# Feed-forward entry of a two-layer decoder: token halves as even and odd tiles, first products in two parts, second weight tile's work reordered

## The chip, the cores and the metric

The kernel runs on one core of a Trainium2 chip. The metric is the device time of one execution in microseconds; the median of the runs is compared, and lower is better. All 1024 tokens and all weights are float32; the products are made from rounded parts (a high part and the remainder) of each operand.

## The reference

Two layers over 1024 tokens of width 1024. The first mixes tokens by pooling, the second by sliding-window attention; what the change touches is the entry of each layer's feed-forward part.

```python
def swiglu(x, w_gate, w_up, w_down):
    return (jax.nn.silu(x @ w_gate) * (x @ w_up)) @ w_down

    for i in range(DEPTH):
        hn = rms_norm(h, mix_pre_g[i])
        ...
        h = h + rms_norm(m, mix_post_g[i])
        f = swiglu(rms_norm(h, ffn_pre_g[i]), w_ff_gate[i], w_ff_up[i], w_ff_down[i])
        h = h + rms_norm(f, ffn_post_g[i])
        gate = jax.nn.sigmoid(rms_norm(h, ple_norm_g[i]) @ w_ple_gate[i])
        h = h + (p[i] @ w_ple_proj[i]) * gate
```

## The kernel before

The token axis has eight tiles of 128 (numbered 0 to 7, in pairs `i` with `p` = 0, 1). All of them stay on chip in `H`. Of the feed-forward part, gate and up projections together are computed by a seven-product scheme of the Strassen kind: the token axis, the contraction axis and gate/up are each cut into halves, and seven products replace eight. Each product (`ffn_product`) takes one form of the weights (A11, A12, A22, S1 to S4; A21 is only a summand) and one form of the activations: b11, b21, b22 are parts of the turned, normed tiles, t1 to t4 are differences of them. A form of the activations has four pieces of 128 tokens, so a product is 4 x 3 matmuls of 512 columns (high x high, high x remainder, remainder x high). A11 and A12 need b11 and b21, that is one token half only; every other form but b22 needs both halves.

The hidden axis of 2816 is walked in 11 groups `g` of two weight tiles `t` (0 and 1). For each group the loop makes seven products per weight tile and then two sets of 14 products of the down projection (`ffn_pe_down`), beside the next group's work. Group 0 has no down projection beside it. The first weight tile (0, 0) is written out by itself (`ffn_pe_first`, `ffn_act_first`, `ffn_dve_first`, `ffn_pool_first`), since its products lie between the last tiles of the stage before.

In that stage (pooling in layer 0, the output projection in layer 1) each tile passes: product on TensorE; squares of the output on ScalarE (`output_squares`, L595); the root on GpSimd; scaling and residual add on VectorE (`add_post`, L473, L476); squares of the residual (`fn_squares`, L493); root on GpSimd (`fn_rms`); norm into `tmp` (`fn_normed`, L507); a turn on TensorE into banks 6 and 7 (`fn_turn`, L518); copies (`fn_raw`), rounding (`fn_hi`) and remainders (`fn_lo`). In the kernel before, tiles 0 to 3 are the first token half and need only copy, rounding and two remainders; tiles 4 to 7 are the second, and each makes on VectorE two differences (L568, L569), a third (L575), b22's remainder (L579) and a fourth difference (L585). So A11 and A12 of the first weight tile can run before tiles 6 and 7 are turned, and all other products wait for tile 7.

The order of work on each engine is the order in the code; engines wait for each other by counted semaphores. TensorE's order at the entry (`ffn_pe_first`): A11, turn of tile 6, A12, turn of tile 7, twelve filler matmuls (`keep_busy`, L841), S3, S2, S1, A22, S4; before it, a priming matmul (L835) in bank 1, 2 and 5 opens each bank that several products add to. `copy_first` copies A11's bank on ScalarE so that A12 and the others may be added to either copy; `copy_m7` copies the bank of S3, `copy_u` that of S2. Then `ffn_pe_tile` does the second weight tile in the order A11, S3, S2, A12, S1, A22, S4.

A weight form is loaded raw by SP (L789), summed where it is a sum (`form_sum`, L1111, VectorE or GpSimd), rounded by ScalarE (`form_hi`, L978), and its remainder taken by VectorE or GpSimd (`form_lo`, L1162), which writes over the raw form. The down weights get four sums (`wd_sums`, L1140 to L1146), rounding (`wd_his`, L990) and remainders (`wd_los`, L1155) on the same engines; the activations that come out of the products get their own forms (`d_sums`, L1206 to L1214; `d_his`; `d_los`, from L1223). The down projection's first product of group 0 (L924) needs all of these. Forms of t are rounded by `t_hi` (L1035) and their remainders made by `t_lo` (L1261).

## Time and profile before

| | us |
|---|---|
| median of 3 runs | 1965.93 |
| lowest, highest | 1965.68, 1967.02 |
| the profiled execution | 1965.92 |
| its span in the profile | 1964.1 |

| engine | busy us | share |
|---|---|---|
| TensorE, matmul | 1917.4 | 98% |
| TensorE, weight load | 1573.6 | 80% |
| VectorE | 1402.6 | 71% |
| ScalarE | 905.4 | 46% |
| GpSimd | 457.5 | 23% |

In rows of a timeline the first number is the start from the beginning of the span, the second the time from the first start to the last end of what the row merges, and in brackets stands how long the engine was idle before it and what released it. Instructions overlap at their ends, so the cost of one in a stream is read from start to start. PE is TensorE, DVE VectorE, ACT ScalarE, POOL GpSimd.

### The profile page before, as it was taken

The page shows a single profiled execution, that of the slowest core. Times are in us where ns is not written, and L with a number is a line of the kernel's source. Part 1 is how long each engine was busy: PE and PEld are TensorE (multiplying, and loading weights), DVE is VectorE, ACT ScalarE, POOL GpSimd, SP SyncE. Part 2 cuts the span into 40 slices and gives each one's busy share as a digit, 9 for nine tenths or more (in the row PEclk, how much of TensorE's full clock was granted, in tenths as well). Part 3 has the DMA queues.
Part 4 walks back from the last instruction along what each step waited for, and adds up shares of the span by engine and source line. Part 5 has one row for each costly group of instructions (what it writes and reads, how often), then busy time and mean ns, then how long its engine had stood idle before and what let it go on. Part 6 is the DMA issues. An engine that isn't in the chain of part 4 may idle for free.

```text
span 1964.1 us, 28703 instructions
## 1 busy us (share of the span) xinstructions
PE 1917.4 (98%) x9198; PEld 1573.6 (80%) x9198; DVE 1402.6 (71%) x2382; ACT 905.4 (46%) x1734; POOL 457.5 (23%) x448
## 2 busy tenths in 40 slices
PE   7899999999999999999999999999999999999998
PEld 7778888888888878888866787788888888888787
DVE  5987777777777786565389658777777777777863
ACT  6744444444444453341178545444444444444531
POOL 2312222222222221010046211212122221222310
PEclk9999999999999999999999999999999999999999
DMA  5333332233333350254200213233333223335201
GB/s 201 108 97 104 91 91 87 76 102 91 107 91 91 92 200 22 78 219 172 86 12 2 66 42 123 71 107 92 98 94 91 86 75 106 91 106 176 99 30 67
DMA packets 222055, 188.50 MB, mean 96 GB/s; under 512 B 12192, under 2 KB 199968, under 8 KB 221984
## 3 DMA queue, kind: packets, MB, share of 16 engines
q1 hardware_dynamic: 217712, 183.38, 29.2%
q10 hardware_dynamic: 4272, 4.21, 0.7%
q8 instruction: 40, 0.66, 0.1%
q14 instruction: 31, 0.25, 0.0%
HBM read 166.58 MB, written 20.97 MB: 95 GB/s over the span
## 4 chain that ended last, share of the span: by engine, by line
PE 89%; DVE 6%; issue 2%; ACT 1%; DMA 1%; POOL 1%; SPq 0%; DVEq 0%; ACTq 0%; POOLq 0%
PE ps L827 14%; PE ps L829 14%; PE ps L828 14%; PE ps L315 7%; PE ps L317 7%; PE ps L316 7%; PE ps L925 7%; PE ps L926 7%; PE ps L924 7%; PE ps L1635 2%; PE ps L1716 1%; PE ps L1689 1%; PE ps L389 1%; PE ps L632 1%; DVE t_lo L1261 1%
## 5 line engine op out<-in xcount | busy, mean ns | idle before, releaser
L1249 DVE TENSOR_TENSOR H<-H,ps 128x512 f32<-128x512 f32 x496 | 328.0, 686 | 112.5 <-PE ps L926 111.7
L1111 POOL TENSOR_TENSOR s_raw<-s_raw,a_raw 128x512 f32<-128x512 f32 x66 | 87.5, 1327 | 766.4 <-DVE s_lo L1162 651.0
L827 PE MATMUL ps<-t_hi,s_hi 128*128 128x512 f32 x528 | 206.4, 391 | 8.1 <-DVE t_lo L1261 5.1
L828 PE MATMUL ps<-t_lo,s_hi 128*128 128x512 f32 x528 | 205.5, 389 | 0.0
L829 PE MATMUL ps<-t_hi,s_lo 128*128 128x512 f32 x528 | 205.5, 389 | 0.0
L1000 ACT ACTIVATE m<-ps 128x512 f32<-128x512 f32 x44 | 26.4, 600 | 265.7 <-PE ps L829 263.3
L827 PE MATMUL ps<-b_hi,a_hi 128*128 128x512 f32 x352 | 137.4, 390 | 0.0
L828 PE MATMUL ps<-b_lo,a_hi 128*128 128x512 f32 x352 | 137.3, 390 | 0.0
L829 PE MATMUL ps<-b_hi,a_lo 128*128 128x512 f32 x352 | 137.2, 390 | 0.0
L924 PE MATMUL ps<-wd_hi,d_ab_hi 128*128 128x512 f32 x336 | 130.7, 389 | 0.0
L925 PE MATMUL ps<-wd_lo,d_ab_hi 128*128 128x512 f32 x336 | 130.7, 389 | 0.0
L926 PE MATMUL ps<-wd_hi,d_ab_lo 128*128 128x512 f32 x336 | 130.7, 389 | 0.0
L827 PEld LDWEIGHTS ps<-t_hi,s_hi 128*128 128x128 f32 x528 | 99.1, 188 | 31.4 <-DVE t_lo L1261 6.8
L829 PEld LDWEIGHTS ps<-t_hi,s_lo 128*128 128x128 f32 x528 | 99.1, 188 | 20.8
L828 PEld LDWEIGHTS ps<-t_lo,s_hi 128*128 128x128 f32 x528 | 99.1, 188 | 20.4
L978 ACT ACTIVATE s_hi<-s_raw 128x512 fp32r<-128x512 f32 x132 | 82.8, 627 | 53.9 <-DVE s_raw L1111 53.9
L1162 POOL TENSOR_TENSOR a_lo<-a_raw,a_hi 128x512 fp32r<-128x512 f32 x60 | 80.8, 1347 | 114.2 <-ACT a_hi L978 114.2
L315 PE MATMUL ps<-w_ple_gate_hi,xt_hi 128*128 128x512 f32 x256 | 101.5, 397 | 1.8 <-DVE w_ple_gate_lo L291 0.8
L317 PE MATMUL ps<-w_ple_gate_hi,xt_lo 128*128 128x512 f32 x256 | 99.9, 390 | 0.0
L316 PE MATMUL ps<-w_ple_gate_lo,xt_hi 128*128 128x512 f32 x256 | 99.7, 389 | 0.0
L941 ACT ACTIVATE ps<-ps 128x512 f32<-128x512 f32 x88 | 51.2, 582 | 97.6 <-PE ps L926 90.8
L1681 POOL TENSOR_TENSOR probs<-probs,recip 128x1024 f32<-128x1024 f32 x32 | 60.6, 1893 | 147.8 <-DVE recip L1673 147.8
(293 smaller groups left out, 5022.8 us busy)
## 6 DMA issues: line engine op xcount, KB each, us to landing
a_raw<-in_w_ff_gate SPq DMA_DIRECT2D x88, 256.0 KB, 2.9
a_raw<-in_w_ff_up SPq DMA_DIRECT2D x88, 256.0 KB, 3.0
s_raw<-in_w_ff_up SPq DMA_DIRECT2D x88, 256.0 KB, 2.9
s_raw<-in_w_ff_gate SPq DMA_DIRECT2D x88, 256.0 KB, 3.1
wd_raw<-in_w_ff_down SPq DMA_DIRECT2D x44, 512.0 KB, 4.3
residual_spill<-H SPq DMA_DIRECT2D x16, 512.0 KB, 2.6
raw<-in_w_ple_gate SPq DMA_DIRECT2D x16, 512.0 KB, 6.0
back<-residual_spill SPq DMA_DIRECT2D x16, 512.0 KB, 5.8
```

The costliest lines, as they stand in the source:

```text
L315: pe.matmul(out_, lhs[0], rhs[0], start=first, stop=False)
L316: pe.matmul(out_, lhs[0], rhs[1], start=False, stop=False)
L317: return pe.matmul(out_, lhs[1], rhs[0], start=False, stop=last)
L827: pe.matmul(ps[:, bank, :], w[0], x[0], start=fresh and k == 0, stop=False, skip_group_check=not fresh)
L828: pe.matmul(ps[:, bank, :], w[0], x[1], start=False, stop=False, skip_group_check=not fresh)
L829: last = pe.matmul(ps[:, bank, :], w[1], x[0], start=False, stop=k == 3, skip_group_check=not fresh)
L924: pe.matmul(ps[:, bank, :], a[0], wd_hi[:, b, :], start=fresh, stop=False, skip_group_check=not fresh)
L925: pe.matmul(ps[:, bank, :], a[0], wd_lo[:, b, :], start=False, stop=False, skip_group_check=not fresh)
L926: pe.matmul(ps[:, bank, :], a[1], wd_hi[:, b, :], start=False, stop=True, skip_group_check=not fresh).then_inc(F["down"], 1)
L978: act.activation(W[name][0][:, :, :], form_raw(name), ACT.Copy).then_inc(F["form_hi"], 1)
L1111: eng.tensor_tensor(form_raw(name), W_RAW[name][:, :, :], form_raw(other) if other != "A21" else W_RAW["A21"][:, :, :], op).then_inc(summe ...
L1249: dve.tensor_tensor(dst, dst, src, ALU.add).then_inc(F["summed"], 1)
```

## The change

The token halves become the even tiles (b11, b21) and the odd tiles (b22 and the differences), so a pair 2i, 2i + 1 completes piece i of each form. For group 0 the orders of products, roundings and remainders are written out for both weight tiles together (`ENTRY`, `ENTRY_HI`, `ENTRY_LO`, from which the semaphore counts follow). A11 and A12 of weight tile (0, 0) and A11 of (0, 1) are done in two parts, three pieces (384 columns) before tile 6 is ready and one piece (128 columns) after it; A12 of (0, 1) follows whole, all before S3. The filler matmuls of this place are gone. The second weight tile uses its own banks (`bank_for`) and, for A11, A12 and the raw S1, its own places (`ahead_hi`, `ahead_lo`, `ahead_raw`), loaded by SP when tile 7's product of the stage before is done. Its remaining products are S2, S3, S1, A22, S4 (`ffn_pe_second`), and on ScalarE and VectorE its own copies, roundings and sums stand ahead of the down weights' (`ffn_act_second`, `ffn_dve_second`). t2 is rounded in one pass instead of two. In layer 0 the squares of tile 7 stand ahead of tile 6's copy, in layer 1 behind it. The additions to `H`, the spills' return, the per-layer-embedding stage and the output follow the new tile order through `rows_of`. The number of products is the same. The diff, cut to its core (lines of white space are left out):

```diff
 ORDER = ("A11", "S3", "S2", "A12", "S1", "A22", "S4")
-ORDER_FIRST = ("A11", "A12", "S3", "S2", "S1", "A22", "S4")
+ENTRY = (("A11 begun", 0), ("A11", 0), ("A12", 0), ("A11", 1), ("A12", 1), ("S3", 0), ("S2", 0), ("S1", 0), ("A22", 0), ("S4", 0),
+         ("S2", 1), ("S3", 1), ("S1", 1), ("A22", 1), ("S4", 1))
...
             pe.wait_ge(FN["xn"], done(n))
-            if 1 <= 2 * i + p <= 4:
-                pe.wait_ge(FN["raw"], 1 + 4 * L + 2 * i + p)
+            if p == 1:
+                pe.wait_ge(FN["raw"], 1 + 4 * L + i + 1)
             else:
                 pe.wait_ge(FN["lo"], free(n))
             for k in range(KD):
...
+            if p == 0:
+                act.activation(piece(t_raw[1], i), ps[:, 6, :], ACT.Copy)
+                act.activation(piece(t_raw[4], i), ps[:, 7, :], ACT.Copy).then_inc(FN["raw"], 1)
             else:
-                act.activation(piece(t_raw[3], n - 4), ps[:, 6, :], ACT.Copy)
-                act.activation(piece(xb["b22"][0], n - 4), ps[:, 7, :], ACT.Copy).then_inc(FN["hi"], 1)
+                act.activation(piece(t_raw[3], i), ps[:, 6, :], ACT.Copy)
+                act.activation(piece(xb["b22"][0], i), ps[:, 7, :], ACT.Copy).then_inc(FN["hi"], 1)
         def fn_hi(act, L, i, p):
-            n = 2 * i + p
-            if n < 4:
-                act.wait_ge(FN["raw"], 1 + 4 * L + n + 1)
-                act.activation(piece(xb["b11"][0], n), piece(t_raw[1], n), ACT.Copy)
-                act.activation(piece(xb["b21"][0], n), piece(t_raw[4], n), ACT.Copy).then_inc(FN["hi"], 1)
+            if p == 0:
+                act.wait_ge(FN["raw"], 1 + 4 * L + i + 1)
+                act.activation(piece(xb["b11"][0], i), piece(t_raw[1], i), ACT.Copy)
+                act.activation(piece(xb["b21"][0], i), piece(t_raw[4], i), ACT.Copy).then_inc(FN["hi"], 1)
         def fn_lo(dve, L, i, p):
             n = 2 * i + p
             dve.wait_ge(FN["hi"], done(TILES * L + n))
-            if n < 4:
+            if p == 0:
                 for form, held in (("b11", 1), ("b21", 4)):
-                    hi, lo = [piece(x, n) for x in xb[form]]
-                    last = dve.tensor_tensor(lo, piece(t_raw[held], n), hi.bitcast(F32), ALU.subtract)
+                    hi, lo = [piece(x, i) for x in xb[form]]
+                    last = dve.tensor_tensor(lo, piece(t_raw[held], i), hi.bitcast(F32), ALU.subtract)
                 last.then_inc(FN["lo"], 1)
             else:
                 fn_two_forms(dve, L, n)
...
+        def as_form(x):
+            return x.rearrange("p a c -> p (a c)").rearrange("p (k c) -> p k c", k=4)
+        ahead_hi = {"A11": as_form(Z["d_ac_hi"][:, :, :]), "A12": as_form(Z["d_ab_lo"][:, 0:2, :])}
+        ahead_lo = {"A11": as_form(Z["d_ac_lo"][:, :, :]), "A12": as_form(Z["d_ab_lo"][:, 2:4, :])}
+        ahead_raw = {"A11": as_form(Z["d_ac_raw"][:, :, :]), "A12": as_form(Z["d_ab_raw"][:, 2:4, :]),
+                     "S1": as_form(Z["s1_ahead"][:, 0:2, :])}
...
+        def bank_for(b, g, t):
+            if is_first(g, t):
+                return 4 if b == 3 else b
+            if is_second(g, t):
+                return 3 if b == 0 else b + 4
+            return b
         m7, up0_last, act_late = Z["m7"], Z["up0_last"], ACT_LATE
...
-                pe.matmul(ps[:, bank, :], w[0], x[1], start=False, stop=False, skip_group_check=not fresh)
-                last = pe.matmul(ps[:, bank, :], w[1], x[0], start=False, stop=k == 3, skip_group_check=not fresh)
-            last.then_inc(F["product"], 1)
-        def ffn_pe_prime(pe, form, *primed):
+                w, x = [y[:, k, :] for y in forms_], [y[:, pieces, k, :] for y in X[name]]
+                pe.matmul(o, w[0], x[0], start=fresh and k == 0, stop=False, skip_group_check=not fresh)
+                pe.matmul(o, w[0], x[1], start=False, stop=False, skip_group_check=not fresh)
+                last = pe.matmul(o, w[1], x[0], start=False, stop=k == 3, skip_group_check=not fresh)
+            if pieces.stop == 4 or (name == "A11" and is_first(g, t)):
+                last.then_inc(F["product"], 1)
+        def ffn_pe_prime(pe, form, pieces, *primed):
             for bank in primed:
-                pe.matmul(ps[:, bank, :], W[form][0][:, 0, :], X[form][0][:, :, 0, :], start=True, stop=True)
+                pe.matmul(ps[:, bank, pieces.start * P:pieces.stop * P], W[form][0][:, 0, :], X[form][0][:, pieces, 0, :],
+                          start=pieces.start == 0, stop=True, skip_group_check=pieces.start > 0)
         def keep_busy(pe, count, bank):
@@ -843,18 +888,34 @@
         def ffn_pe_first(pe, L):
             g, t, s = 0, 0, S[("pool", "o")[L]]
+            early, late = slice(0, 3), slice(3, 4)
             pe.wait_ge(*ready("A11", L, g, t))
+            pe.wait_ge(FN["lo"], done(TILES * L + 4))
             if L == 1:
                 pe.wait_ge(FN["ssum"], done(TILES * L + TILES - 2))
-            ffn_pe_prime(pe, "A11", 1)
-            ffn_product(pe, "A11", L, g, t)
-            fn_turn(pe, L, PAIRS - 1, 0)
+            if L == 1:
+                fn_turn(pe, L, PAIRS - 1, 0)
+            ffn_pe_prime(pe, "A11", early, 1)
+            ffn_product(pe, "A11", L, g, t, early)
             pe.wait_ge(s["added"][0], s.done("added", PAIRS - 1))
-            ffn_pe_prime(pe, "A12", 2)
+            pe.wait_ge(*ready("A12", L, g, t))
+            ffn_pe_prime(pe, "A12", early, 2)
+            pe.wait_ge(F["copied"], copied_early(L))
+            ffn_product(pe, "A12", L, g, t, early)
+            if L == 0:
+                fn_turn(pe, L, PAIRS - 1, 0)
+            ffn_product(pe, "A11", L, 0, 1, early)
+            pe.wait_ge(FN["lo"], done(TILES * L + TILES - 2))
+            ffn_pe_prime(pe, "A12", late, 1, 2)
+            ffn_product(pe, "A11", L, g, t, late)
+            pe.wait_ge(s["added"][1], s.done("added", PAIRS - 1))
+            ffn_pe_prime(pe, "A12", slice(0, 4), 5)
+            fn_turn(pe, L, PAIRS - 1, 1)
             pe.wait_ge(F["copied"], nth_copy(0, L, g, t))
-            ffn_product(pe, "A12", L, g, t)
-            fn_turn(pe, L, PAIRS - 1, 1)
-            keep_busy(pe, 12, 3)
+            ffn_product(pe, "A12", L, g, t, late)
+            ffn_product(pe, "A11", L, 0, 1, late)
+            pe.wait_ge(F["copied"], nth_copy(0, L, 0, 1))
+            ffn_product(pe, "A12", L, 0, 1)
             pe.wait_ge(F["t"], 4 * L + 1)
             ffn_product(pe, "S3", L, g, t)
             pe.wait_ge(F["t"], 4 * L + 2)
@@ -866,8 +927,19 @@
             ffn_product(pe, "A22", L, g, t)
             pe.wait_ge(FN["lo"], done(TILES * L + TILES - 1))
             pe.wait_ge(F["up1"], 1 + tau(L, g, t) + 1)
-            pe.wait_ge(*ready("S4", L, g, t))
-            ffn_pe_prime(pe, "S4", 5)
+            ffn_product(pe, "S4", L, g, t)
+        def ffn_pe_second(pe, L):
+            g, t = 0, 1
+            pe.wait_ge(*ready("S2", L, g, t))
+            ffn_pe_prime(pe, "S2", slice(0, 4), 6)
+            for name in ("S2", "S3"):
+                ffn_product(pe, name, L, g, t)
+            pe.wait_ge(F["copied"], nth_copy(2, L, g, t))
+            for name in ("S1", "A22"):
+                ffn_product(pe, name, L, g, t)
+            pe.wait_ge(F["up1"], 1 + tau(L, g, t) + 1)
             ffn_product(pe, "S4", L, g, t)
...
@@ -1022,24 +1108,35 @@
         def ffn_act_first(act, L):
             g, t = 0, 0
-            copy_first(act, L, g, t)
+            if L == 1:
+                fn_raw(act, L, PAIRS - 1, 0)
+            copy_first(act, L, g, t, "A11 begun")
             if L == 0:
                 first_hi(act, L)
-            fn_raw(act, L, PAIRS - 1, 0)
+                form_hi(act, "A11", L, 0, 1)
+            else:
+                fn_hi(act, L, PAIRS - 1, 0)
             fn_squares(act, L, PAIRS - 1, 1)
+            if L == 0:
+                fn_raw(act, L, PAIRS - 1, 0)
+                fn_hi(act, L, PAIRS - 1, 0)
+            else:
+                form_hi(act, "A11", L, 0, 1)
+            form_hi(act, "A12", L, 0, 1)
+            copy_first(act, L, g, t)
             def t_hi(m, pieces):
-                n = pieces.stop + 3
+                n = 2 * pieces.stop - 1
                 act.wait_ge(t_step, steps_of(L, n) + {3: 1, 1: 2, 2: 3, 4: 4}[m])
                 act.activation(xb[f"t{m}"][0][:, pieces, :, :], t_raw[m][:, pieces, :, :], ACT.Copy
                                ).then_inc(F["t_hi"], 1)
-            for m in (3, 2):
-                t_hi(m, slice(0, 3))
+            t_hi(3, slice(0, 3))
             fn_raw(act, L, PAIRS - 1, 1)
-            for m in (3, 2):
-                t_hi(m, slice(3, 4))
+            copy_first(act, L, 0, 1)
+            t_hi(3, slice(3, 4))
+            t_hi(2, slice(0, 4))
             t_hi(1, slice(0, 4))
             form_hi(act, "A22", L, g, t)
             copy_m7(act, L, g, t)
@@ -1048,13 +1145,12 @@
             form_hi(act, "S4", L, g, t)
             gate_silu(act, L, g, t, 0)
             n = following(g, t)
-            for name in ("A11", "S3", "S2", "A12", "S1"):
+            for name in ("S3", "S2", "S1"):
                 form_hi(act, name, L, *n)
         def ffn_act_tile(act, L, g):
-            t, p, n, down = 0, preceding(g, 0), following(g, 0), g - 1
-            gate_silu(act, L, *p, 1)
+            t, n, down = 0, following(g, 0), g - 1
             form_hi(act, "S2", L, g, t)
             d_his(act, L, down, 0)
...
+            if is_second(g, t):
+                copy_u(act, L, g, t)
+                copy_m7(act, L, g, t)
+                form_hi(act, "A22", L, g, t)
+                form_hi(act, "S4", L, g, t)
+                wd_his(act, L, g, range(4))
+            else:
+                wd_his(act, L, g, (0, 1))
+                copy_first(act, L, g, t)
+                form_hi(act, "A22", L, g, t)
+                wd_his(act, L, g, (2, 3))
+                copy_m7(act, L, g, t)
+                form_hi(act, "S4", L, g, t)
+                copy_u(act, L, g, t)
             if not is_last(g, t):
                 form_hi(act, "A11", L, *n)
             gate_silu(act, L, g, t, 0)
             if not is_last(g, t):
                 form_hi(act, "S3", L, *n)
+                gate_silu(act, L, g, t, 1)
...
                                          ALU.subtract)
             last = steps_of(L, TILES - 1)
+            if L == 0:
+                form_lo(dve, "A11", L, 0, 1)
             fn_lo(dve, L, PAIRS - 1, 0)
+            if L == 1:
+                form_lo(dve, "A11", L, 0, 1)
             fn_normed(dve, L, PAIRS - 1, 1)
+            form_lo(dve, "A12", L, 0, 1)
             if L == 0:
                 form_lo(dve, "S3", L, g, t)
-            fn_fourth_form(dve, L, TILES - 2)
             t_lo(3, slice(0, 3), 1, last)
             dve.wait_ge(FN["hi"], done(TILES * L + TILES - 1))
             fn_two_forms(dve, L, TILES - 1)
-            t_lo(3, slice(3, 4), 3, last + 1).then_inc(F["t"], 1)
+            t_lo(3, slice(3, 4), 2, last + 1).then_inc(F["t"], 1)
             fn_second_form(dve, L, TILES - 1)
             fn_fourth_form(dve, L, TILES - 1)
             if L == 0:
                 form_lo(dve, "S2", L, g, t)
-            t_lo(2, slice(0, 4), 4, last + 4).then_inc(F["t"], 1)
+            t_lo(2, slice(0, 4), 3, last + 4).then_inc(F["t"], 1)
             if L == 0:
                 form_lo(dve, "S1", L, g, t)
-            t_lo(1, slice(0, 4), 5, last + 4).then_inc(F["t"], 1)
...
+            if is_second(g, t):
+                times_up(dve, L, *p, 1)
+                form_sum(dve, "S4", L, g, t)
+                form_lo(dve, "A22", L, g, t)
+                wd_sums(dve, L, g)
+                form_lo(dve, "S4", L, g, t)
+                up_second_half(dve, L, g, t)
+                wd_los(dve, L, g, (0, 1))
+                up_first_half(dve, L, g, t)
+                times_up(dve, L, g, t, 0)
+                form_lo(dve, "A11", L, *n)
+                form_sum(dve, "S3", L, *n)
+                wd_los(dve, L, g, (2, 3))
+                form_sum(dve, "S1", L, *n)
+                form_sum(dve, "S2", L, *n)
+                form_lo(dve, "S3", L, *n)
+                d_sums(dve, L, g, 0)
+                return
             wd_sums(dve, L, g)
             times_up(dve, L, *p, 1)
...
+            return 2 * (slot % 4) + slot // 4
+        def slot_rows(i, p):
+            return bass.ds(rows_of(2 * i + p) * D, D)
         def of_tile(work, L):
...
+                sp.wait_ge(s["used"][1], s.done("used", PAIRS - 1))
+                ffn_load(sp, "A11", "a11", L, 0, 1)
+                ffn_load(sp, "A12", "a12", L, 0, 1)
                 spill_tile(5)
                 spill_tile(6)
+                sp.wait_ge(s["added"][1], s.done("added", PAIRS - 1))
+                ffn_load(sp, "S4", "a12", L, *first)
                 sp.wait_ge(FN["ssum"], done(TILES * L + TILES - 1))
                 ffn_load(sp, "A22", "a22", L, *first)
+                sp.wait_ge(F["form_loaded"]["S1"], 16 * (tau(L, 0, 0) + 1))
+                ffn_load(sp, "S1", "a22", L, 0, 1)
                 spill_tile(TILES - 1)
-                ffn_load(sp, "S4", "a12", L, *first)
                 ffn_load_down(sp, L, 0)
                 for t in range(2):
                     ffn_load_tile(sp, L, 0, t)
```

## Rows read from the trace of the kernel before

**Rows 1.** The page's head and its part on busy time.

```profile
span 1964.1 us, 28703 instructions
...
PE 1917.4 (98%) x9198; PEld 1573.6 (80%) x9198; DVE 1402.6 (71%) x2382; ACT 905.4 (46%) x1734; POOL 457.5 (23%) x448
```

**Rows 2.** TensorE's waits over the span: releaser, total us, times, longest.

```profile
engine line waited for: us in total, times, longest us
...
PE ps L518 <- DVE tmp L507: 6.5, 4, 2.7
...
PE ps L827 <- DVE t_lo L1261: 5.1, 5, 1.3
```

**Rows 3.** Timeline, TensorE, layer 0's entry: start us, us, instruction, idle before.

```profile
80.14 1.67 PE L518 MATMUL ps<-ident,tmp 128*128 128x128 f32 x8 [2.68 <-DVE tmp L507]
...
86.91 1.10 PE L518 MATMUL ps<-ident,tmp 128*128 128x128 f32 x8 [1.09 <-DVE tmp L507]
...
87.85 2.84 PE L841 MATMUL ps<-ident 128*128 128x128 f32 x24
...
91.97 0.50 PE L827 MATMUL ps<-t_hi,s_hi 128*128 128x512 f32 x1 [1.28 <-DVE t_lo L1261]
...
115.45 0.50 PE L827 MATMUL ps<-t_hi,s_hi 128*128 128x512 f32 x1 [0.94 <-ACT ps L1005]
...
126.48 0.39 PE L827 MATMUL ps<-b_hi,s_hi 128*128 128x512 f32 x1
...
134.64 0.39 PE L924 MATMUL ps<-wd_hi,d_ac_hi 128*128 128x512 f32 x1
```

**Rows 4.** Timeline, TensorE, layer 1's entry.

```profile
1201.55 1.09 PE L518 MATMUL ps<-ident,tmp 128*128 128x128 f32 x8 [2.17 <-DVE tmp L507]
...
1210.31 0.50 PE L827 MATMUL ps<-t_hi,s_hi 128*128 128x512 f32 x1 [0.67 <-DVE t_lo L1261]
...
1214.04 0.47 PE L827 MATMUL ps<-t_hi,s_hi 128*128 128x512 f32 x1 [0.72 <-issue]
...
1248.64 0.39 PE L924 MATMUL ps<-wd_hi,d_ac_hi 128*128 128x512 f32 x1
```

**Rows 5.** A stretch of TensorE, layer 0: length, PE busy, granted clock, DMA.

```profile
80.00:83.70 3.70, 3.56 (x13) 0.57 0.00 0
```

**Rows 6.** Timelines, VectorE and ScalarE, layer 1's entry.

```profile
1196.56 1.22 DVE L476 TENSOR_TENSOR H<-H,ps 128x1024 f32<-128x1024 f32 x1
...
1197.88 1.07 ACT L493 ACTIVATE o_junk<-H 128x1024 f32<-128x1024 f32 x1 [0.33 <-DVE H L476]
...
1198.93 2.84 ACT L1035 ACTIVATE t_hi<-t_raw 128x1536 fp32r<-128x1536 f32 x2
...
1207.97 4.49 DVE L1261 TENSOR_TENSOR t_lo<-t_raw,t_hi 128x2048 fp32r<-128x2048 f32 x2
```

**Rows 7.** Timeline, VectorE, layer 1, second weight tile.

```profile
1225.38 0.69 DVE L1140 TENSOR_TENSOR wd_raw<-wd_raw 128x512 f32<-128x512 f32 x1
...
1228.11 0.69 DVE L1189 TENSOR_TENSOR act_late<-m,act_late 128x512 f32<-128x512 f32 x1
...
1230.58 2.35 DVE L1155 TENSOR_TENSOR wd_lo<-wd_raw,wd_hi 128x1024 fp32r<-128x1024 f32 x2
...
1232.85 0.68 DVE L1111 TENSOR_TENSOR s_raw<-s_raw,a_raw 128x512 f32<-128x512 f32 x1
...
1233.45 1.82 DVE L1155 TENSOR_TENSOR wd_lo<-wd_raw,wd_hi 128x1024 fp32r<-128x1024 f32 x2
...
1242.08 0.69 DVE L1111 TENSOR_TENSOR s_raw<-s_raw,a_raw 128x512 f32<-128x512 f32 x1
...
1244.28 0.42 DVE L1206 TENSOR_TENSOR d_ac_raw<-d_ab_raw 128x256 f32<-128x256 f32 x1
...
1246.47 0.69 DVE L1223 TENSOR_TENSOR d_ac_lo<-d_ac_raw,d_ac_hi 128x512 fp32r<-128x512 f32 x1
```

**Rows 8.** Timelines, VectorE and GpSimd, layer 0.

```profile
62.03 1.29 DVE L507 SCALAR_TENSOR_TENSOR tmp<-H,small,gain 128x1024 f32<-128x1024 f32 x1 [1.08 <-POOL small L501]
...
93.98 3.22 POOL L1111 TENSOR_TENSOR s_raw<-s_raw,a_raw 128x512 f32<-128x512 f32 x1 [8.69 <-issue]
```

166 lines of the change are left out of this document (94 added, 72 removed), and 3 rows, old and new, of the table ENTRY_LO.

## The prediction

> **What bounds the kernel now.** I read the busy times first, then TensorE's waits, then the timeline around both entries of the feed-forward part, then the two engines that feed it. TensorE has work for 1917.4 of 1964.1 us [rows 1], so about 47 us of idle time is all that a reordering can win; a change here must be judged by TensorE's start times. The waits put two of the larger sums at the entry: the turns of the normed tiles (6.5 us in four waits) and the products on the combined forms (5.1 us) [rows 2]. The timeline shows the same picture in both layers. In layer 0 the turn of tile 6 waits 2.68 us and that of tile 7 1.09, twelve filler matmuls (24 instructions) run for 2.84, S3 waits another 1.28, and the second weight tile stalls 0.94 on a copy [rows 3]. In layer 1 tile 7's turn waits 2.17 [rows 4]. From 126.48 to 134.64 TensorE does three products without a gap [rows 3]: 2.72 us per product of twelve 512-column matmuls, 0.227 each. That stretch ends in the first product of the down projection, and so I take its start (134.64 and 1248.64) as the finish line: behind it the loop is untouched.
>
> **The change: what leaves TensorE's path.** Pairing even with odd tiles makes the combined forms late by one quarter only, and A11 and A12 can start on three quarters. The filler is gone, A11 and A12 of the second weight tile (5.44 us) move up in front of S3, and the second tile's stall goes, since S2 now opens it and S3 covers the copy. If these were all, layer 1 would win some 6 us. Each step must be followed to what is late next, because the added work is itself waiting for something.
>
> **The entry in layer 1.** Up to the residual add of tile 7 nothing on the path moves; that add starts at 1196.56 and is 1.22 long, so it ends at 1197.78 [rows 6].
> 1. Squares of tile 7: 0.10 later, 1.15 with the accumulator read, to 1199.03 (before: 1197.88 to 1198.93) [rows 6]. Only then does ScalarE round A11 of tile two, 0.6, and VectorE takes the remainder, 0.7 with the hand-over: ready at 1200.35.
> 2. TensorE has by then done turn 6, A11 and A12 on three quarters, and stands from about 1198.4: a wait of 2 us that replaces the 2.17 in front of the turn.
> 3. A11 of tile two on 384 columns: 12 x 0.17 (three quarters of 0.227) = 2.04. Then 14 matmuls of 128 columns. No row has this form; the nearest is the filler, also 128 wide and with its own weight loads, 24 in 2.84 = 0.118 [rows 3], against a floor of a quarter of 0.227 and a ceiling of the whole. I take 0.12, since the filler's weight loads are of the same size: 1.7. A priming matmul 0.23. The turn of tile 7 starts at 1204.3, where it was 1201.55 [rows 4]: 2.75 later.
> 4. ScalarE copies the last quarter of A11 and rounds three quarters of t3 (half of 2.84 [rows 6]) before it reads the turn: its copy ends at 1207.0. VectorE: the rest of t3's remainder, two differences 1.2, then t3's last quarter 0.7 behind a rounding of 0.6, the third difference at 1210.6.
> 5. t2 was rounded in two parts, so that only a quarter (0.5) stood on the path; now all four quarters are one pass behind the last tile, 1.85, and its remainder 2.25 (two of that size took 4.49 [rows 6]). S2 can start at 1214.95, where it was 1210.31 [rows 4]: 4.64 later. TensorE's own order (12 + 12 narrow, A12 of tile two, S3) ends at 1214.3, so the two chains are nearly equal and one replaces the other.
> The price of moving the loads: A11 and A12 of tile two are issued when tile 7's product has read its operands, 3 us or more before they are rounded, so no one waits for them; the two spills that SP now issues behind them are needed only at the first down additions. The sum for S4 on GpSimd waits for S2's remainder; the loads of A21 and S3 are queued behind it on SP, and are wanted 10 us later.
>
> **The second weight tile.** From S2: to S1 3.73 as before (1210.31 to 1214.04 [rows 4]), then S1, A22, S4 8.2, restart and priming 0.3, S2 and S3 of tile two 5.45, drain 0.15: S3 ends 17.85 after S2's start, at 1232.8. By TensorE alone S1, A22, S4 and the next group's A11 and S3 follow, 13.6, and the down product would start at 1246.4, 2.2 earlier than before.
> But the vector side no longer keeps up. ScalarE copies S3's bank before it rounds A22, so VectorE's remainder of A22 waits for the end of S3 plus 1.18; and everything of the down weights is queued behind that remainder on VectorE, where before the four sums of wd began at 1225.38, ahead of it [rows 7]. From there: remainder of A22, of S4, up's second half, the next A11 and the sum S3, five passes of 0.60; up's first half and its product 1.4; the sums of wd 2.73 (1225.38 to 1228.11); remainders of wd 2.27 for four slots (1230.58 to 1232.85) and 1.7 for three; sums S1, S2 and remainder of S3 2.2 (1242.08 to 1244.28) [rows 7]. That is 13.3. The forms of the activations and the first remainder add 2.9 (1244.28 to 1246.47, plus 0.69) [rows 7]. So the down product starts 1.18 + 13.3 + 2.9 = 17.4 behind S3's end, not 13.6: at 1250.2, against 1248.64. On the way the next A11 waits about 2 us and the next S3 about 1.7. Layer 1: +1.6.
>
> **The entry in layer 0.** The odd tiles' four passes now fall on tiles 1 and 3. Tile 1's go into waits; tile 3's 2.5 us meet a wait of 1.08 [rows 8], so the last pool product starts 0.5 later, and tile 7's residual add, with the reordered tail, ends at 83.9 in place of 83.1. Then the order differs: squares to 85.2, and only behind them the copy and rounding of tile 6 (1.0 + 1.1) to 87.3, its remainders 1.2 to 88.6, A11's last quarter to 90.35, turn 7 at 90.6 (it was 86.91 [rows 3]); then the same chain as above, to a remainder of t2 that starts at 98.8. GpSimd's sum for S4 now comes in front of that one; in the profile it shared the ports for 3.22 us [rows 8], undisturbed sums take 1.3, and I charge 0.6 (bounds 0 and 1.9). S2 at 101.75, the down product 35.4 later (17.85 + 17.4, and 0.15 because this layer's S1 restarts slower): 137.2, against 134.64 [rows 3]. Layer 0: +2.6. TensorE's clock fell to 0.57 of full speed, near the lower of its two levels (1.2 GHz), after the wait of 2.68 [rows 5]; there are again waits of 2 to 2.7 us, but the slowed matmuls would lie ahead of another wait (for tile 6's remainders), so I charge nothing; uncovered it costs up to 1.8.
>
> **Sum.** The profiled execution took 1965.92 us, equal to the median of 1965.93, with 1.8 of it outside the span. 1965.9 + 1.6 + 2.6 = 1970.1. All else (the PLE part and the output in another tile order, the loads back, the key and value stage, whose tile k needs a slot no later than k + 3) is the same number of instructions with slack, and I cost it at nothing.
>
> The Trainium skill ("TensorE: Matmul & The Clock Gate", Back-to-back issue gap) gives about 81 ns for a 128-column matmul in a stream of weight load and matmul. No row here has such a matmul of this data type. By that figure turn 7 comes 0.55 earlier in each layer, and the sum would be 1969.0.
>
> **Rivals.**
> A, the forecast: VectorE bounds the second tile, 1970.1; its own range is 1967 to 1972. For it: the program order of the two queues leaves no choice. Chance 0.47.
> B, narrow matmuls cost as much as wide ones: 0.227 at 128 columns. Turn 7 then comes 1.5 later, and the 24 behind it take 2.6 more, so that TensorE's own order gets ahead of t2; S2 is 3.4 later in each layer: 1970.1 + 6.8 = 1976.9. Against it: the filler's 0.118. Chance 0.18.
> C, the faster side: VectorE keeps up in the second tile. It decides whether A22's rounding really waits for S3's end; if A22's remainder comes 3.9 us sooner, TensorE's 13.6 counts. Then layer 1 ends 2.2 earlier than before and layer 0 1.4 earlier: 1965.9 - 3.6 = 1962.3. For it: VectorE has over 2 us of waiting in that stretch. Against it: both queues are strict in order. Chance 0.17.
> D, the entry is shorter than I sum, by 2 us a layer, while the second tile stays bound: 1966. For it: my chain has some twenty hand-overs. Chance 0.18.
>
> **How the numbers follow.** The predicted time is A's, 1970.1. The range 1962.3 to 1977 takes in C's and B's times and leaves their outer halves out, about 2 in 10. A measurement of this kernel tells 0.2% (3.9 us) from no change. Slower by more than that (over 1969.9): 0.28 of A and all of B but a little, 0.46. Faster (under 1962.0): half of C and a little of D, 0.12. Within: the rest, 0.42.
>
> **What the new profile would show.** Right: the first down product near 137 and 1250; idle time of 1.5 to 2 us in front of the next group's A11 and again S3, released by VectorE; in front of A11 of tile two a wait of 2 to 3 us; the turns of tile 7 near 90.6 and 1204.3. The price of 128 columns can be read from start to start. Wrong would be: a second tile without waits (C), or the last quarter of A11 taking 2.7 us (B).

## Result and the profile after

The changed kernel takes 1972.62 us, the median of six executions (1970.18 to 1975.68); the kernel before took 1966.26 beside it (1965.68 to 1967.02). The ratio is 1.0032, with a 95% interval of 1.0022 to 1.0043: 6.4 us slower. The forecast was 1970.1. The profiled execution is the fastest of the six, 1970.18, with a span of 1968.3 against 1964.1 [rows 1]. So the result has two parts that must be read apart: 4.2 us that the profile holds, and a spread upwards that it does not. Five more executions of the same kernel took 1972.67 to 1975.56.

The page of the changed kernel, busy times, and TensorE's waits (releaser, total us, times, longest); they answer to [rows 1] and [rows 2]:

```profile
PE 1919.2 (98%) x9228; PEld 1576.6 (80%) x9228; DVE 1404.5 (71%) x2382; ACT 905.0 (46%) x1734; POOL 453.6 (23%) x448
...
PE ps L870 <- DVE d_ac_lo L1268: 4.1, 2, 2.5
PE ps L870 <- DVE s_lo L1268: 3.0, 2, 1.5
...
PE ps L870 <- DVE a_lo L1268: 2.5, 2, 1.3
...
PE ps L870 <- DVE t_lo L1367: 1.4, 2, 1.0
...
PE ps L528 <- DVE tmp L517: 0.5, 2, 0.3
```

The 6.5 us in front of the turns are down to 0.5, and the 5.1 in front of the combined forms to 1.4. In their place stand 4.1 us in front of A11 of tile two (`d_ac_lo` holds its lower half; I call a form's rounded part its upper half and the remainder its lower half), and 3.0 and 2.5 us in front of the next group's S3 and A11.

TensorE's timeline, changed kernel, layer 0 and then layer 1 (start us, us, instruction, idle before and its releaser), beside [rows 3] and [rows 4]:

```profile
80.98 1.04 PE L528 MATMUL ps<-ident,tmp 128*128 128x128 f32 x8
84.54 0.45 PE L870 MATMUL ps<-b_hi,d_ac_hi 128*128 128x384 f32 x1 [2.52 <-DVE d_ac_lo L1268]
84.83 0.34 PE L871 MATMUL ps<-b_lo,d_ac_hi 128*128 128x384 f32 x1
85.00 0.35 PE L872 MATMUL ps<-b_hi,d_ac_lo 128*128 128x384 f32 x1
...
85.75 0.52 PE L872 MATMUL ps<-b_hi,d_ac_lo 128*128 128x384 f32 x1
86.07 0.52 PE L870 MATMUL ps<-b_hi,d_ac_hi 128*128 128x384 f32 x1
...
88.66 0.44 PE L879 MATMUL ps<-b_hi,a_hi 128*128 128x128 f32 x2 [0.47 <-DVE b_lo L562]
88.94 0.27 PE L870 MATMUL ps<-b_hi,a_hi 128*128 128x128 f32 x1
89.05 0.28 PE L871 MATMUL ps<-b_lo,a_hi 128*128 128x128 f32 x1
...
90.56 1.04 PE L528 MATMUL ps<-ident,tmp 128*128 128x128 f32 x8
...
101.67 0.50 PE L870 MATMUL ps<-t_hi,s_hi 128*128 128x512 f32 x1 [1.04 <-DVE t_lo L1367]
...
129.68 0.50 PE L870 MATMUL ps<-b_hi,a_hi 128*128 128x512 f32 x1 [1.23 <-DVE a_lo L1268]
134.21 0.50 PE L870 MATMUL ps<-t_hi,s_hi 128*128 128x512 f32 x1 [1.48 <-DVE s_lo L1268]
137.11 0.39 PE L996 MATMUL ps<-wd_hi,d_ac_hi 128*128 128x512 f32 x1
```

```profile
1194.99 1.04 PE L528 MATMUL ps<-ident,tmp 128*128 128x128 f32 x8
...
1202.87 0.45 PE L870 MATMUL ps<-b_hi,d_ac_hi 128*128 128x384 f32 x1 [1.63 <-DVE d_ac_lo L1268]
1206.88 1.03 PE L528 MATMUL ps<-ident,tmp 128*128 128x128 f32 x8
1217.36 0.50 PE L870 MATMUL ps<-t_hi,s_hi 128*128 128x512 f32 x1 [0.39 <-DVE t_lo L1367]
1252.81 0.39 PE L996 MATMUL ps<-wd_hi,d_ac_hi 128*128 128x512 f32 x1
```

The finish lines move from 134.64 [rows 3] to 137.11, +2.47, and from 1248.64 [rows 4] to 1252.81, +4.17, of which 1.70 arise in layer 1. That is the whole difference of the spans.

Between executions, layer 0 starts some tenths earlier or later. So below I count from the turn of tile 6 to the first down product of the same layer: 56.13 us in layer 0 (80.98 to 137.11) and 57.82 in layer 1 (1194.99 to 1252.81) in the changed kernel. I call them the stretches.

VectorE's timeline, changed kernel, layer 0, second weight tile:

```profile
116.91 0.69 DVE L1216 TENSOR_TENSOR s_raw<-s_raw,a_raw 128x512 f32<-128x512 f32 x1 [1.67 <-DMA s_raw<-in_w_ff_gate]
120.73 0.69 DVE L1268 TENSOR_TENSOR a_lo<-a_raw,a_hi 128x512 fp32r<-128x512 f32 x1 [3.13 <-ACT a_hi L1050]
...
136.26 0.69 DVE L1329 TENSOR_TENSOR d_ac_lo<-d_ac_raw,d_ac_hi 128x512 fp32r<-128x512 f32 x1
```

VectorE stands still for 3.13 us in front of A22's lower half and then has no gap until the forms of the activations at 136.26: the down product cannot start before that.

### The profile page after: what moved, and what is told of

Same layout as the page of the kernel before. It is cut to its first block, busy times and chain, and to the rows that moved or that the text cites. A ratio compares the mean times of both kernels' runs of the same rounds, so it can differ in the third digit from the quotient of the medians.

```text
span 1968.3 us, 28728 instructions
## 1 busy us (share of the span) xinstructions
PE 1919.2 (98%) x9228; PEld 1576.6 (80%) x9228; DVE 1404.5 (71%) x2382; ACT 905.0 (46%) x1734; POOL 453.6 (23%) x448
## 4 chain that ended last, share of the span: by engine, by line
PE 89%; DVE 6%; ACT 2%; issue 2%; POOL 1%; DMA 0%; POOLq 0%; DVEq 0%; ACTq 0%
PE ps L870 14%; PE ps L872 14%; PE ps L871 14%; PE ps L325 7%; PE ps L327 7%; PE ps L326 7%; PE ps L998 7%; PE ps L997 7%; PE ps L996 7%; PE ps L1769 2%; PE ps L1850 1%; PE ps L1823 1%; PE ps L399 1%; PE ps L641 1%; DVE w_ple_gate_lo L301 1%
## 5 line engine op out<-in xcount | busy, mean ns | idle before, releaser
L870 PE MATMUL ps<-b_hi,a_hi 128*128 128x512 f32 (+2 forms) x352 | 134.8, 383 | 4.0 <-DVE a_lo L1268 2.5
L871 PE MATMUL ps<-b_lo,a_hi 128*128 128x512 f32 (+2 forms) x352 | 134.3, 382 | 0.0
L872 PE MATMUL ps<-b_hi,a_lo 128*128 128x512 f32 (+2 forms) x352 | 134.3, 382 | 0.0
```

The lines of the kernel that those rows point to most:

```text
L870: pe.matmul(o, w[0], x[0], start=fresh and k == 0, stop=False, skip_group_check=not fresh)
L871: pe.matmul(o, w[0], x[1], start=False, stop=False, skip_group_check=not fresh)
L872: last = pe.matmul(o, w[1], x[0], start=False, stop=k == 3, skip_group_check=not fresh)
```

## Experiments: VectorE's queue in the second weight tile

My theory: in the second tile, what counts is VectorE's queue, and it starts late because ScalarE copies S3's bank ahead of rounding A22. The rival was that copies and SiLU on ScalarE are the chain and VectorE only follows.

**e1.** The rounding of A22 goes ahead of both copies that wait for TensorE, that of S4 ahead of the copy of S3's bank.

```
 if is_second(g, t):
+    form_hi(act, "A22", L, g, t)
     copy_u(act, L, g, t)
-    copy_m7(act, L, g, t)
-    form_hi(act, "A22", L, g, t)
     form_hi(act, "S4", L, g, t)
+    copy_m7(act, L, g, t)
     wd_his(act, L, g, range(4))
```

> In the second tile ScalarE rounds A22 ahead of both PSUM copies, and S4 ahead of the copy from S3's bank; the order of VectorE and TensorE stays. Theory M (between S3 of tile two and the first down product VectorE's queue is the bound, and it stands still 3.1 us in each layer in front of A22's second half because ScalarE reaches A22's first half only after S3's copy): the wait of VectorE before A22's lower half goes from 3.1 to under 0.5 us, the waits before the next A11 and the next S3 (1.2 and 1.5 us) vanish, the first down products come 2.5 to 3 us earlier in each layer (at 134.1 to 134.6 in layer 0), and the time is 5 to 6 us below that of the changed kernel, at or below the kernel before. Rival C' (VectorE only waits for what is late anyway, the bound is ScalarE's own chain of copy and SiLU): the wait moves, the down products come within 0.5 us of 137.1 and 1252.8.

Measured: median 1969.32, from 1965.62 to 1971.41 over eleven executions. Its profile, VectorE in layer 0 and TensorE in layer 1:

```profile
122.08 0.69 DVE L1216 TENSOR_TENSOR s_raw<-s_raw,a_raw 128x512 f32<-128x512 f32 x1 [1.58 <-DMA s_raw<-in_w_ff_gate]
122.69 0.68 DVE L1268 TENSOR_TENSOR a_lo<-a_raw,a_hi 128x512 fp32r<-128x512 f32 x1
```

```profile
1198.14 1.04 PE L528 MATMUL ps<-ident,tmp 128*128 128x128 f32 x8
...
1250.67 0.50 PE L870 MATMUL ps<-t_hi,s_hi 128*128 128x512 f32 x1 [1.43 <-DVE s_lo L1268]
1253.52 0.44 PE L996 MATMUL ps<-wd_hi,d_ac_hi 128*128 128x512 f32 x1
```

The 3.1 us of standing still are gone, and layer 1's stretch goes from 57.82 to 55.38: 2.44 less, a little under the 2.5 to 3 expected, since VectorE now waits 0.75 us for TensorE in front of up's second half. Layer 0 of this execution ran at a low clock (below), so its stretch, 58.68, can't be compared. The fastest execution is at 1965.62, 4.6 below the changed kernel's; I had expected 5 to 6. The theory holds against its rival, with one part wrong: the wait in front of the next A11 vanished, that in front of the next S3 (1.43) stayed. The order of two queues in the second tile is thus worth more than the 4.2 us by which the change is slower.

**e5.** On top of e1, VectorE's sums of the down weights go ahead of S4's sum, where it waited 1.58 us for a load. The first rounding of them (two slots) goes on ScalarE ahead of the copy of S3's bank, and its remainder on VectorE ahead of up's second half.

```
 form_hi(act, "S4", L, g, t)
+wd_his(act, L, g, (0,))
 copy_m7(act, L, g, t)
-wd_his(act, L, g, range(4))
+wd_his(act, L, g, (1, 2, 3))
...
-form_sum(dve, "S4", L, g, t)
-form_lo(dve, "A22", L, g, t)
 wd_sums(dve, L, g)
+form_sum(dve, "S4", L, g, t)
+form_lo(dve, "A22", L, g, t)
 form_lo(dve, "S4", L, g, t)
+wd_los(dve, L, g, (0,))
 up_second_half(dve, L, g, t)
-wd_los(dve, L, g, (0, 1))
+wd_los(dve, L, g, (1,))
 up_first_half(dve, L, g, t)
```

> On top of the ScalarE order of e1, VectorE forms the sums of the down weights ahead of S4's sum of tile two, where it waited 1.6 us for a load, and ScalarE and VectorE round the first two of them ahead of S3's copy and the last sum of the tile. Theory M (in the second tile VectorE's queue is the bound to the end, and each us that it stands still ahead of it is worth a us): the wait before the next S3, 1.4 us in both layers in e1, falls under 0.4, the first down product of layer 1 comes 1.1 to 1.4 us earlier than in e1 counted from the turn of tile 6 (55.4 to about 54.1 us), and the fastest executions go from 1965.6 to about 1963. Rival (the wait before S3 is set by SiLU and the sums behind it): it stays at 1.4. The spread of 5 us from the clock stays.

Measured: median 1967.23 (1964.81 to 1970.51), stretch of layer 1 55.27, so 0.1 less and not 1.1 to 1.4; the wait before the next S3 is 1.28. (The medians of e1 and e5 differ by 2.1 us, but both kernels spread over more than 5, so I go by the stretches.) Its VectorE, layer 0:

```profile
124.12 0.69 DVE L1279 TENSOR_TENSOR act_late<-ps,m 128x512 f32<-128x512 f32 x1 [0.82 <-PE ps L872]
...
126.84 0.69 DVE L1285 TENSOR_TENSOR m<-ps,m 128x512 f32<-128x512 f32 x1 [0.89 <-PE ps L872]
```

This was a miss that taught the limit of the theory. VectorE now waits for TensorE twice, 0.82 and 0.89 us. What it did early only lengthened these; the chain from the sum behind A22's product (here at 126.84) to the down product has the same length as in e1, 9.5 us in layer 1 of both.

**e8.** Built on e7 (below): the remainder of one more batch of the down weights (two slots) moves on VectorE ahead of the sum on A22's product.

```
-wd_los(dve, L, g, (1,))
+wd_los(dve, L, g, (1, 2))
 up_first_half(dve, L, g, t)
...
-wd_los(dve, L, g, (2, 3))
+wd_los(dve, L, g, (3,))
```

> e7 with one of the four down-weight roundings of VectorE (1.2 us as timed in pairs, 0.6 each behind one another) moved ahead of the sum of A22's bank, where VectorE in e7 stands still 0.89 us. e5 showed that emptying the queue ahead of S3's copy gave 0.1 us and not 1.2, since VectorE then waits for A22's product and the chain from there to the next S3 is unchanged. Theory M' (only what stands behind A22's product counts there): 0.6 us less behind it, the wait before the next S3 from 1.28 to about 0.7, 1.2 us less in all: 1960.8. Rival (the later SiLU product makes the next A11 late in its place): a wait appears before the next A11 and the time is that of e7.

Measured: median 1959.91 (1959.19 to 1961.60, seven executions), against 1961.98 of e7. TensorE and VectorE of e8, layer 0:

```profile
127.71 0.50 PE L870 MATMUL ps<-t_hi,s_hi 128*128 128x512 f32 x1 [0.29 <-DVE s_lo L1271]
130.57 0.44 PE L997 MATMUL ps<-wd_hi,d_ac_hi 128*128 128x512 f32 x1
```

```profile
119.91 2.35 DVE L1263 TENSOR_TENSOR wd_lo<-wd_raw,wd_hi 128x1024 fp32r<-128x1024 f32 x2
122.17 0.69 DVE L1287 TENSOR_TENSOR m<-ps,m 128x512 f32<-128x512 f32 x1
```

The idle 0.89 is filled, no new wait appears, and the wait before the next S3 goes from 1.28 to 0.29; the stretches are 0.97 and 1.01 us shorter than e7's (layer 1: 54.84 to 53.83), 2.0 together, as the medians say. I had counted the moved batch at 0.6; it is two slots, 1.2 us, of which the idle took 0.9.

## Experiments: the entry

**e4.** The prediction put t2's rounding in one pass at the heart of S2's delay. Here it is in two instructions.

```
-t_hi(2, slice(0, 4))
+t_hi(2, slice(0, 3))
+t_hi(2, slice(3, 4))
```

The counts that VectorE waits for follow from it.

> The changed kernel with the upper half of t2 rounded in two instructions (three pieces of four first, the last one when tile 7 is in), as t3 is; nothing else moves. Theory M (the prediction's step that t2 in one pass delays S2): the first piece runs in ScalarE's gap ahead of 96.7, t2's lower half starts about 1.2 us earlier, the waits before S2 (1.04 us in layer 0, 0.39 in layer 1) vanish and the first down products come that much earlier: 1.4 us off the executions with a held clock, 1970.2 to about 1968.8. Rival (VectorE is busy there anyway, so an earlier upper half buys nothing): both waits stay within 0.2 us and so does the time. The spread of 1970 to 1975 is not touched.

Measured: median 1970.71, fastest 1968.44, and six of eleven executions at 1968.4 to 1970.7; the other five reach 1977.41. t2's lower half on VectorE in layer 0, in the changed kernel and then in e4:

```profile
98.69 2.92 DVE L1367 TENSOR_TENSOR t_lo<-t_raw,t_hi 128x2048 fp32r<-128x2048 f32 x1 [0.66 <-ACT t_hi L1132]
```

```profile
97.84 2.29 DVE L1368 TENSOR_TENSOR t_lo<-t_raw,t_hi 128x2048 fp32r<-128x2048 f32 x1
```

It starts 0.85 us earlier. It is also 0.63 shorter, which is a second cause beside the one that the edit was meant for: in the changed kernel GpSimd's sum for S4 starts first (98.16) and takes 1.30, in e4 it starts second (98.06) and takes 3.21. The waits before S2 are gone in both layers, and the stretches are 54.96 and 57.34, 1.17 and 0.48 less. The step holds: S2 follows t2. In layer 0 the gain is not the single pass alone; in layer 1, with no sum beside it, it is.

**e3.** In layer 0, tile 6 is copied and rounded ahead of tile 7's squares.

```
-fn_squares(act, L, PAIRS - 1, 1)
 if L == 0:
     fn_raw(act, L, PAIRS - 1, 0)
     fn_hi(act, L, PAIRS - 1, 0)
-else:
+fn_squares(act, L, PAIRS - 1, 1)
+if L == 1:
     form_hi(act, "A11", L, 0, 1)
```

> In layer 0 alone ScalarE copies and rounds tile 6 ahead of the squares of tile 7, as the kernel before had it. Theory M (the prediction's step: the squares ahead of the copy move tile 6's lower halves, then the turn of tile 7, then S2): lower halves of tile 6 from 87.3 to about 85.5, the turn of tile 7 from 90.56 to 89.5 to 89.9, S2 and the first down product 0.6 to 1.0 us earlier, the time 0.6 to 1.0 us less than the changed kernel's. Rival (S2's release does not hang on the turn of tile 7 but on TensorE's own products ahead of it): S2 stays within 0.2 of 101.67 and the time is the same.

Measured: median 1969.86, from 1968.85 to 1970.49 over eleven executions, where the changed kernel spreads over 5.5 us. TensorE of e3, layer 0:

```profile
87.20 0.33 PE L879 MATMUL ps<-b_hi,a_hi 128*128 128x128 f32 x2
...
89.00 1.03 PE L528 MATMUL ps<-ident,tmp 128*128 128x128 f32 x8
...
135.80 0.40 PE L996 MATMUL ps<-wd_hi,d_ac_hi 128*128 128x512 f32 x1
```

The stretch (81.46 to 135.80) is 54.34, 1.79 less, more than the 0.6 to 1.0 expected; the profiled execution, which starts 0.5 us later at the turn of tile 6, took 1968.85, 1.3 less. The reason is in the first row: tile 6's lower halves are in before A11 of tile two ends, so the quarter-width products no longer wait. That wait turned out to matter for the clock too.

## Experiments: the clock and the spread

The prediction charged the clock nothing and put it at 1.8 us if uncovered. Below, the first wait is the one in front of A11 of tile two, and the second wait the one behind it, for tile 6's lower halves, in front of the quarter-width products. **e0** is the changed kernel itself, profiled in another execution.

> The changed kernel itself, unedited. What is open: its six times before this lay between 1970.2 and 1975.7 us, and the longer ones went with a mean granted clock of 0.996 to 0.997 against 0.999. Theory M (the forecast's sum: longer waits at the entry of each FFN, +4.2 us, is all that is fixed; on top of it the TensorE clock falls in some executions): again times at 1970 to 1971 and others at 1974 to 1976, each with the lower clock, and a profile whose first down products are at 137.1 and 1252.8 where the clock held. Theory N (the spread is something of that one chip): all times within 1 us.

Measured: median 1973.45 (1972.67 to 1975.56, five executions), so no execution near 1970 this time. Its TensorE, and then the windows of the changed kernel, of e0 and of e1 (length, PE busy, granted clock, DMA):

```profile
88.91 0.44 PE L879 MATMUL ps<-b_hi,a_hi 128*128 128x128 f32 x2 [1.77 <-DVE b_lo L562]
...
138.97 0.40 PE L996 MATMUL ps<-wd_hi,d_ac_hi 128*128 128x512 f32 x1
```

```profile
85.00:88.00 3.00, 3.00 (x11) 0.54 0.73 199
88.00:91.00 3.00, 2.53 (x21) 0.89 1.05 342
```

```profile
85.00:88.00 3.00, 2.13 (x12) 1.00 0.67 192
88.00:91.00 3.00, 2.10 (x13) 0.79 1.05 316
91.00:94.00 3.00, 3.00 (x18) 0.64 0.70 284
```

```profile
85.00:88.00 3.00, 3.00 (x12) 0.68 0.65 179
88.00:91.00 3.00, 2.06 (x11) 0.50 1.03 336
```

In the first two, the clock is at its lower level (1.2 GHz, half) for 3.4 us in all, twice the share that is missing from 1.00 times the length. In the first execution it fell at 85.2, inside A11 of tile two; the slowed products ended just ahead of tile 6's lower halves, so the loss was hidden. In the second it held through those products, TensorE stood still once more for 1.77 us, and the clock fell at 89.8, on the quarter-width products, where nothing covers it: stretch 57.76, 1.6 more. In e1 it fell at 86.1, ahead of the second wait (0.94 us there), and came back at 103.1, 17 us later.

**e2 and e9** put filler matmuls into the first wait, in front of A11 of tile two: 20 calls in layer 0 and 12 in layer 1 in e2, as shown, and 10 and none in e9.

```
     fn_turn(pe, L, PAIRS - 1, 0)
+keep_busy(pe, (20, 12)[L], 3)
 ffn_product(pe, "A11", L, 0, 1, early)
```

> TensorE is kept busy in its wait before the narrow A11 of tile two: 20 small products (2.4 us at the 0.118 us of the kernel's own filler) in layer 0 and 12 in layer 1, nothing else moved. Theory K (the idle stretch of 2.5 us in front of A11 of tile two is what lets the clock fall, and the longer executions are those where the fall lasts): the granted clock of 85 to 91 us is 1.0 instead of 0.54 to 0.9, all clocks are at 0.999 or above, and the median goes from 1972.6 to about 1970 with under 1 us between the lowest and the highest. In the profiled execution the gain is near nothing, since the copied halves of tile 6 are late there anyway. Rival (the clock falls elsewhere or at random): the spread of 5 us stays and the median with it.

> The changed kernel with filler of 2.2 us in layer 0 alone, inside its 2.5 us wait before the narrow A11 of tile two; layer 1 untouched. Theory K (the whole spread, and the part of the median above the forecast, is the clock after that one idle stretch): all executions at 1970.0 to 1970.8, within 1 us, clock 0.999 or above; the first down product of layer 0 stays at 137.1. Rival (layer 1's waits take part, or the entry is faster with a clock at full speed): executions above 1971.5 remain, or the down product comes over 0.5 us earlier than 137.1.

Measured: e2 has a median of 1971.71 and all eight executions within 1.2 us (1971.54 to 1972.69), the clock at 1.00 all through layer 0's entry. A call is two matmuls and 0.22 us, so the filler outran the wait: layer 1's stretch is 58.46, 0.64 more. Layer 0's stretch, without any fall, is 56.04 against 56.13 in the changed kernel's profile, so there the fall did cost almost nothing. e9, with filler that fits, has a median of 1974.62 (1970.76 to 1975.51). Its TensorE and its windows:

```profile
84.48 0.44 PE L870 MATMUL ps<-b_hi,d_ac_hi 128*128 128x384 f32 x1 [0.28 <-DVE d_ac_lo L1269]
88.60 0.44 PE L879 MATMUL ps<-b_hi,a_hi 128*128 128x128 f32 x2 [1.75 <-DVE b_lo L562]
...
141.75 0.44 PE L997 MATMUL ps<-wd_hi,d_ac_hi 128*128 128x512 f32 x1
```

```profile
88.00:91.00 3.00, 2.40 (x14) 0.69 1.04 362
91.00:94.00 3.00, 3.00 (x15) 0.50 0.63 247
...
97.00:100.00 3.00, 2.33 (x10) 0.50 0.00 0
100.00:104.00 4.00, 4.00 (x13) 0.65 0.00 0
```

So my theory that the first wait alone is the cause falls. It is filled in e9, and the clock still falls behind the second wait (1.75 us), here for 13.7 us; the stretch is 60.82, 4.7 more, which is the whole of this execution's excess (span 1973.0 against 1968.3). In e2 the long filler had pushed A11 of tile two up to tile 6's arrival, so the second wait was gone, and so was the spread.

The kernels divide by that second wait. With it, lowest to highest: 5.5 us in the changed kernel, 2.9 in e0, 5.8 in e1, 9.0 in e4, 5.7 in e5, 4.8 in e9, 5.8 in e10. Without it: 1.2 in e2, 1.6 in e3, 1.7 in e6, 2.0 in e7, 2.4 in e8. The mean granted clock, which is known for every execution, divides them as well: with the second wait 29 of 60 executions have 0.994 to 0.997, without it none of 48 is below 0.998. In a span of 1968 us, 3.4 us at half speed take 0.001 off this mean and 13.7 us take 0.0035 (an estimate from these lengths), so long falls are what the second wait goes with. Only the profiles of e1 and e9 show where a long fall lies.

Short falls are there without the second wait too: 3.4 us from 93.6 in e3, and 3.4 us from 85.2 in e6, where nothing covers them and the turn of tile 7 comes 9.12 us after that of tile 6, against 7.54 in e3. And e3 and e6 keep the whole first wait (2.51 us) with a small spread. So the first wait is neither needed (e9) nor enough (e3, e6) for the spread; removing the second, by filler (e2) or by order (e3), was enough both times.

**e10** is e9's filler with e1's order.

> e9's filler and e1's ScalarE order. With the clock held, the difference from e9 is what ScalarE's order in the second tile costs: 2.4 us in layer 1, as e1's profile showed (turn of tile 6 to first down product 57.8 to 55.4), and 2.2 in layer 0: 1965.4 to 1965.9 and within 1 us, level with the kernel before. Rival (the two effects are not apart: e1's fast executions were fast by chance of the clock alone): 1967 or more.

Measured: median 1967.87 (1965.26 to 1971.01). Its profile has the same 3.4 us of low clock at 88 to 94 as e0's, and its stretches are 55.32 and 55.40, against 57.76 in e0 and 57.82: 2.4 less in each layer. So the two effects add in the stretches. By its times alone it was a miss: I expected 1965.4 to 1965.9 within 1 us, and 1967 or more was the rival's sign. The spread is the one of kernels with the second wait (1.76 us here), which e9's filler leaves in place.

**e11** was to ask whether the kernel before loses to its clock at 80 to 83.7 [rows 5].

> The kernel before, with 2.4 us of filler in layer 0 in its wait of 2.68 us before the turn that its profile shows at 80.14, after which its clock was at 0.57 for 3.7 us. Theory K' (the kernel before loses clock too, but VectorE's late t3, which ends the wait at 91.97, hides it): the clock is 1.0 there, the products from 82.03 on end earlier, S3 and S2 start within 0.3 us of 91.97 and 96.10, the median stays within 0.4 us of 1966.2. Rival (the kernel before pays for its clock as well): over 1 us less.

Measured: median 1967.29 (1966.67 to 1968.16), 1.0 more. I had put the filler one turn too early: it ran at 72.87 for 2.6 us ahead of tile 5's turn, which had 0.57 us to wait, and pushed everything behind it (down product 136.10 in place of 134.64). The clock also fell in other places than in the kernel before: in layer 0 from 87.5 us and in layer 1 from 1203.7, for 3.4 us each. So the run does not separate the excess of the filler from the clock, and what the fall of the clock costs the kernel before stays open.

## Experiments: together

**e6** is e5 and e3 together; **e7** adds e4 and filler of ten and six calls.

> e5 and e3 together: second tile reordered, and in layer 0 tile 6 copied ahead of tile 7's squares. If the two gains are of separate stretches they add: fastest executions at about 1961.8 (1963 less the 1.3 of layer 0). In e3 the long low clock did not appear in any of 11 executions; if it is the length of the stretch of late work in layer 0 that lets it stay low, the spread is under 2 us here too and the median is at 1962 to 1963. If that was chance, executions at 1966 and above show up.

> e6 with t2 in two parts and with filler in the waits before the narrow A11 of tile two: 10 calls in layer 0 and 6 in layer 1. In e2 a call turned out to take 0.22 us (two passes of 0.11), so its 20 and 12 calls were longer than the waits of 2.5 and 1.65 us and cost 0.6 us in layer 1; these are 2.2 and 1.3 us. Theory K (that idle stretch lets the clock fall): granted clock 1.0 from 80 to 106 us, all executions within 1 us, median at or 0.4 below the fastest of e6. Rival (the filler costs what it gives): median above that of e6.

Measured: e6 1965.11 (1963.94 to 1965.67), the small spread as expected, the level 2 us above it, since e5's gain was not there. e7 1961.98 (1961.33 to 1963.35), 3.1 less: 2.7 in layer 0, where the clock is now 1.00 throughout and t2 comes in parts, 0.4 in layer 1. Of the 2.7, e4's part was 1.2; the rest, 1.5, goes with the clock: the turn of tile 7 comes 7.56 us after that of tile 6, against 9.12 in e6. The filler alone (e9) did not hold it. With e8 the kernel is at 1959.91, a ratio of 0.9971 to the kernel before (0.9960 to 0.9982): 6.4 us faster, where the change as made is 6.4 slower.

## Why the prediction was right, and where it was not

- *Finish lines*: 137.2 and 1250.2 forecast as shifts of 2.6 and 1.6; measured 2.47 and 1.70. The sum, 1970.1, is the profiled execution's 1970.18. That this execution was the fastest of six is chance: e0's profiled one took 1972.67, and the median, 1972.62, is 2.5 above the forecast. e1 shows the mechanism itself, not only its total.
- *Layer 0's entry*: lower halves of tile 6 to 88.6 and turn 7 at 90.6, measured 90.56; S2 at 101.75, measured 101.67. The step that S2 follows t2's single pass is confirmed by e4 (waits of 1.04 and 0.39 gone). The 0.6 charged for GpSimd's sum is there too: t2's lower half took 2.92 us in place of 2.29.
- *Layer 1's entry*: A11 of tile two waits 1.63, forecast 2. The turn of tile 7 is at 1206.88; less the 2.47 brought from layer 0 that is 1204.4, forecast 1204.3.
- *Second tile*: next A11 and S3 wait 1.2 and 1.5, forecast 2 and 1.7. Not forecast was a wait of 0.42 in front of S4, for VectorE's sum behind S1. A22's lower half waits for S3's copy, as the step said (gone in e1).
- *Narrow matmuls (B)*: 0.11 us from start to start at 128 columns (88.94 to 89.05), where I took 0.12; at 384 columns 0.17, as taken. B falls. The Trainium skill ("TensorE: Matmul & The Clock Gate", Back-to-back issue gap) has about 81 ns for 128 columns; the 128-column matmuls of this kernel take 0.11 at full clock, and the sum by its figure, 1969.0, is not what came.
- *VectorE keeps up (C)*: falls for the kernel as it is. Built in e1, it gives 2.4 us a layer and not the 3.8 that separate 17.4 from 13.6, since VectorE is then held by the chain behind A22's product (e5, e8).
- *A shorter entry (D)*: not seen; the entries came out within 0.2 us of the sum.
- *The step that failed: "so I charge nothing; uncovered it costs up to 1.8"*. In the profiled execution the cover was real (56.13 against 56.04 without a fall, e2). In e0's the clock held through the products that are covered and fell on those that are not, which cost 1.6 us, as the bound of 1.8 says; in e9's it stayed low for 13.7 us, which cost 4.7 and breaks that bound. I had forecast the wait for tile 6's lower halves and used it as cover, but did not see that it is itself a second idle stretch in front of uncovered work. The executions without a profile fit: those of this kernel at 1974.1 and above have a mean granted clock of 0.996 or 0.997, those up to 1971.0 one of 0.999. I put the excess of the medians down to that term: 2.4 us (1972.62 against 1970.18), and 3.3 in e0's five. That is argued from the mean clocks; only profiled executions show the stretch itself.

Not settled: why the low clock lasts 3.4 us in some executions and 13.7 (e9) or 17 (e1) in others, and why it falls inside A11 of tile two in some and behind it in others.

## What to carry to other kernels

When work is pulled ahead on the bound engine, go through the queues that feed it: an instruction that waits for the bound engine (here a copy out of its bank) must not stand ahead of one that could have run before, and of the work behind it only what follows the last hand-over counts. A wait that covers slowed work is also an idle stretch in front of the next work. Where a kernel has such a wait, one profile may show the lucky case; take the spread of several executions before a median is explained.
